# A second modulation mat-vec moved from the Fourier stage into the input projection's tail, and a regrouped Fourier stage

## The reference, cut to what matters

```python
mod_lat = silu(c) @ w_mod + b_mod              # 6*D wide; the first 2*D are needed at once (shift, scale of norm 1)
mod     = silu(c_2) @ w_ada_2 + b_ada_2        # 6*D wide, for the second block

prj = modulate(rmsnorm(x, norm1), sh1, sc1) @ w_in           # z, xbc, dt, f
z, xbc, dt, f = split_proj(prj)
y   = ssd_mixer(z, xbc, dt, ...)                             # conv, silu, scan
fg  = f.reshape(b, l, 4, 128)
spec = fft2(fg, axes=(1, 3), norm='ortho').real              # over 1024 tokens and 128 channels
four = einsum('blgc,gcd->blgd', spec, w_four)
x = x + g1 * (concatenate([y, four]) @ w_out)
```

## Time and profile before

| | before |
|---|---|
| median of 3 runs | 3131.88 us |
| lowest and highest run | 3130.84 and 3138.63 us |
| span of the profiled execution (first to last instruction) | 3136.6 us |
| PE, PEld, DVE, ACT, POOL busy | 90%, 60%, 39%, 20%, 7% |
| mean granted TensorE clock | 0.944 of full speed |

### The profile page before, as it was taken

The page is one execution under the profiler, slowest core; times in us unless marked ns, Lnnn a source line. Parts: engine busy times, 40 slices in busy tenths (PEclk is TensorE's granted clock), DMA queues, the critical chain, the costliest instruction groups (busy, mean ns, idle before and its releaser), DMA issues. The chain is left out here.

```text
span 3136.6 us, 36957 instructions
## 1 busy us (share of the span) xinstructions
PE 2816.6 (90%) x14094; PEld 1878.9 (60%) x14094; DVE 1226.3 (39%) x1848; ACT 639.7 (20%) x1057; POOL 231.0 (7%) x242
## 2 busy tenths in 40 slices
PE   4999996987798899999998599799888899999998
PEld 2888775762576545445544487687666645445444
DVE  3666317885524311111113564673442611111113
ACT  4322323641302000000002422233120200000002
POOL 0000000000000000000002121121000000000002
PEclk6999997998999899999999699899898899999999
DMA  6642226779735799999996413453653699999995
GB/s 246 242 163 71 74 76 198 222 226 422 269 111 204 286 408 410 409 411 406 412 411 227 114 48 108 81 122 111 228 188 130 273 388 412 409 409 406 409 410 215
DMA packets 294747, 812.65 MB, mean 259 GB/s; under 512 B 38364, under 2 KB 160760, under 8 KB 232432
## 3 DMA queue, kind: packets, MB, share of 16 engines
q1 hardware_dynamic: 248864, 702.45, 60.1%
q10 hardware_dynamic: 30640, 62.81, 5.5%
q0 software_dynamic: 15136, 45.91, 4.2%
HBM read 693.18 MB, written 117.91 MB: 259 GB/s over the span
## 5 line engine op out<-in xcount | busy, mean ns | idle before, releaser
L710 PE MATMUL m_ps_y<-m_wa,m_hTa 128*128 128x512 f32 x560 | 255.5, 599 | 0.0
L689 PE MATMUL m_ps_ga<-m_wa,m_xTa 128*128 128x512 f32 x560 | 253.0, 605 | 1.1 <-issue 1.1
L699 PE MATMUL m_ps_b<-m_wb,m_xTb 128*64 128x256 f32 x2240 | 249.5, 381 | 0.0
L689 PE MATMUL m_ps_ua<-m_wa,m_xTa 128*128 128x512 f32 x560 | 246.0, 592 | 0.0
L1145 PE MATMUL xp_acc<-xp_xh,xp_wh 128*128 128x512 f32 (+3 forms) x600 | 223.0, 372 | 6.7 <-DVE xp_xl L1419 6.7
L1146 PE MATMUL xp_acc<-xp_xl,xp_wh 128*128 128x512 f32 (+3 forms) x600 | 221.2, 369 | 0.0
L1147 PE MATMUL xp_acc<-xp_xh,xp_wl 128*128 128x512 f32 (+3 forms) x600 | 221.1, 368 | 0.0
L699 PEld LDWEIGHTS m_ps_b<-m_wb,m_xTb 128*64 128x64 f32 x2240 | 157.8, 137 | 102.3 <-issue 26.5
L812 DVE TENSOR_TENSOR m_hida<-m_ps_ua,m_sila 128x512 f32<-128x512 f32 x35 | 24.2, 691 | 471.1 <-PE m_ps_ua L689 471.1
L780 ACT ACT_TABLE_LOAD x35 | 44.9, 1283 | 756.3 <-PE m_ps_ga L689 675.7
L2379 PE MATMUL xq_acc<-xq_xh,xq_wh 128*128 128x512 f32 x448 | 180.7, 403 | 13.5 <-DVE xq_xl L2801 8.4
(11 more groups left out here) (553 smaller groups left out, 4455.1 us busy)
## 6 DMA issues: line engine op xcount, KB each, us to landing
m_wa<-in_w_dram SPq DMA_DIRECT2D x102, 1024.0 KB, 11.3
m_wb<-in_w_dram SPq DMA_DIRECT2D x102, 1024.0 KB, 12.0
m_wa<-in_w_eg_dram SPq DMA_DIRECT2D x36, 1024.0 KB, 13.1
m_wa<-in_w_eu_dram SPq DMA_DIRECT2D x36, 1024.0 KB, 11.5
m_wb<-in_w_eg_dram SPq DMA_DIRECT2D x36, 1024.0 KB, 11.2
m_wb<-in_w_eu_dram SPq DMA_DIRECT2D x36, 1024.0 KB, 14.6
m_wa<-in_w_ed_dram SPq DMA_DIRECT2D x36, 1024.0 KB
m_wb<-in_w_ed_dram SPq DMA_DIRECT2D x36, 1024.0 KB, 16.1
```

Source lines behind the costliest of these rows:

```text
L689: last = nc.tensor.matmul(out[:, :], xT_a[:, j, :], w[:, k, :], start=(j == 0), stop=(j == J - 1))
L699: last = nc.tensor.matmul(ps_b[c * SB:(c + 1) * SB, p // 2, :], xT_b[:, j, :], w[:, k, c * HF:(c + 1) * HF], start=(j == 0), stop=(j == J ...
L710: last = nc.tensor.matmul(ps_y[:, d * NF:(d + 1) * NF], hT_a[:, k, :], w[:, c, d * NF:(d + 1) * NF], start=(k == 0), stop=(k == JF - 1))
```

## The change

The mat-vec leaves `fourier`, and `mod_tiles` is gone. In `mixer1_in` it is done in ten chunks of 1024 columns (`MC`), eight 128x1024 tiles (512 KB) each, through a ring of four (`MR`). The ring, three accumulators (`macc`) and the result rows (`mrow`) use the SBUF space of the convolution's buffers, which are free after n = 17. For chunk c (M0 = 18):

- SP issues its eight loads in iteration n = 21 + c, after `weights(n)` (`mod_weights`); at n = 21 it also issues eight small bias loads (`mod_biases`); chunks 8 and 9 follow after the loop, then the writes of `a_dram`, then eight stores and the wait for them (`mod_store`). POOL clears `mrow`.
- ACT multiplies the first tile with its silu(c) column (`mod_first`) after the drains of n = 18 + c.
- VectorE adds the other seven, one SCALAR_TENSOR_TENSOR 128x1024 each (`mod_rest`), at the end of iteration n = 18 + c. Each waits for the one before.
- PE sums over the partitions with four matmuls 128x256 against a column of ones (`mod_summed`) after the first group of n = 21 + c, and VectorE adds the bias to the sum (`mod_biased`) in iteration n = 22 + c, before that iteration's `mod_rest`.

The step sizes and decay sums of `mixer1_in` come one iteration earlier (n = 17 and 20 on ACT and VectorE, PE's `sums` at n = 19).

`fourier` loads f by channel group with a semaphore each, loads the twiddle table last and waits for it only ahead of the second matmuls. The first matmuls go group by group in halves of t. The butterflies are done in two halves of 256 columns, each after its own two groups; the copies that turned `t = 6` by -i and the two 128x4096 copies at the end are folded into the operand choice and the sign of `rot`. The second matmuls go by group: 8 x 2 for one group into one of two PSUM slots of 128x1024, then one ACT copy and one VectorE subtraction of 128x1024.

```diff
@@ mixer1_in
+    M0 = Z0 + 1
+        MC, MR, MA = 1024, 4, 3
+        groups = [(k, g) for k, part in enumerate(mod_parts) for g in range(part[1].shape[1] // MC)]
+        NM2 = len(groups)
+        mring, macc, mrow = sb("mring", [P, MR, MC]), sb("macc", [P, MA, MC]), sb("mrow", [P, NM2, MC // NQ4])
...
+        def conv_buffers_free(eng):
+            eng.wait_ge(s_cv, NM)
+            eng.wait_ge(s_xc, NM)
+            eng.wait_ge(s_tq, Q_DT + 1)
+            for r in range(4):
+                eng.wait_ge(s_to[r], 16 * len(range(r, 3 * NT, 4)))
...
+                conv_buffers_free(pool)
+                nc.gpsimd.memset(mrow[:, :, :], 0.0).then_inc(s_mz, 1)
...
+                def mod_weights(c):
+                    k, g = groups[c]
+                    w_m = mod_parts[k][1].rearrange("(p j) n -> p j n", j=J)
+                    if c == 0:
+                        conv_buffers_free(sp)
+                    for j in range(J):
+                        i = J * c + j
+                        if i >= MR:
+                            d, e = divmod(i - MR, J)
+                            if e == 0:
+                                sp.wait_ge(s_m1, d + 1)
+                            else:
+                                sp.wait_ge(s_mf, (J - 1) * d + e)
+                        sp.dma_start(mring[:, i % MR, :], w_m[:, j, g * MC:(g + 1) * MC]).then_inc(s_mw[i % MR], 16)
...
                 for n in range(2, NCH):
                     weights(n)
...
+                    if n >= M0 + 3:
+                        mod_weights(n - M0 - 3)
+                    if n == M0 + 3:
+                        mod_biases()
+                for c in range(NCH - M0 - 3, NM2):
+                    mod_weights(c)
...
                 sp.wait_ge(s_ad, 32)
+                mod_store()
...
+                def mod_summed(c):
+                    pe.wait_ge(s_mf, (J - 1) * (c + 1))
+                    if c < 2:
+                        pe.wait_ge(s_te, Q_SUM + 2 + c)
+                    else:
+                        pe.wait_ge(s_me, c - 1)
+                    n = MC // NQ4
+                    for q in range(NQ4):
+                        last = nc.tensor.matmul(mod_sum(c)[q * CG:q * CG + 1, :], ONE[:, 0:1], macc[:, c % MA, q * n:(q + 1) * n],
+                                                start=True, stop=True)
+                    last.then_inc(s_mr, 1)
...
                 for n in range(2, NCH):
                     for g in range(3 if n <= DT else 2):
                         product(n, g)
+                        if g == 0 and n >= M0 + 3:
+                            mod_summed(n - M0 - 3)
...
-                    if n == DT + 4:
+                    if n == DT + 3:
                         sums()
...
+                def mod_first(c):
+                    i = J * c
+                    if c == 0:
+                        act.wait_ge(s_msg, 1)
+                    act.wait_ge(s_mw[i % MR], 16 * (i // MR + 1))
+                    if c >= MA:
+                        act.wait_ge(s_mr, c - MA + 1)
+                    k = groups[c][0]
+                    nc.scalar.activation(macc[:, c % MA, :], mring[:, i % MR, :], ACT.Copy, scale=msg[:, k, 0:1]).then_inc(s_m1, 1)
...
+                def mod_rest(c):
+                    k = groups[c][0]
+                    v.wait_ge(s_m1, c + 1)
+                    for j in range(1, J):
+                        i = J * c + j
+                        v.wait_ge(s_mw[i % MR], 16 * (i // MR + 1))
+                        nc.vector.scalar_tensor_tensor(out=macc[:, c % MA, :], in0=mring[:, i % MR, :], scalar=msg[:, k, j:j + 1],
+                                                       in1=macc[:, c % MA, :], op0=ALU.mult, op1=ALU.add).then_inc(s_mf, 1)
+                        v.wait_ge(s_mf, (J - 1) * c + j)
...
                     if n + 2 < NCH:
                         low(n + 2)
-                    if n == DT + 2:
+                    if n == DT + 1:
                         step_sizes()
-                    if n == DT + 5:
+                    if n == DT + 4:
                         decay_values()
                     if n == DT + 7:
                         sums_out()
+                    if n >= M0 + 4:
+                        mod_biased(n - M0 - 4)
+                    if n >= M0 and n - M0 < NM2:
+                        mod_rest(n - M0)
+                for c in range(NCH - M0 - 4, NM2):
+                    mod_biased(c)
@@ fourier
-                sp.dma_start(rt[:, :, :, :], rot).then_inc(s_in, 16)
-                sp.dma_start(fT[:, :, :], f_dram).then_inc(s_f, 16)
-                mod_load(sp)
-                mod_store(sp)
+                for g in range(G):
+                    sp.dma_start(fT[:, g, :], f_dram[:, g, :]).then_inc(s_f[g], 16)
+                sp.dma_start(rt[:, :, :, :], rot).then_inc(s_rt, 16)
...
+                for g in range(G):
+                    pe.wait_ge(s_f[g], 16)
+                    for h in range(2):
+                        u = 2 * g + h
+                        if u >= 2:
+                            pe.wait_ge(s_ev, 2 * (u - 1))
+                        for i in range(T // 2):
+                            t = h * (T // 2) + i
+                            last = nc.tensor.matmul(p_u[:, u % 2, i, :, :], fT[:, g, t * P:(t + 1) * P], cw[:, g, :, :],
+                                                    start=True, stop=True)
+                        last.then_inc(s_u, 1)
+                pe.wait_ge(s_rt, 16)
+                for g in range(G):
+                    pe.wait_ge(s_g, g * NB // G + 1)
+                    if g >= 2:
+                        pe.wait_ge(s_ol, g - 1)
+                    for k2 in range(T):
                         for a in range(2):
-                            last = nc.tensor.matmul(p_f[:, k2 % 2, g, :], ab[:, a, k2, g * P:(g + 1) * P], rt[:, a, k2, :],
+                            last = nc.tensor.matmul(p_f[:, g % 2, k2, :], bb[:, a, k2, g * P:(g + 1) * P], rt[:, a, k2, :],
                                                     start=(a == 0), stop=(a == 1))
                     last.then_inc(s_o, 1)
...
+                def butterflies(n):
+                    v.wait_ge(s_ev, 4 * G // NB * (n + 1))
+                    x, y = (z[:, :, :, n * CB:(n + 1) * CB] for z in (ab, bb))
+                    for c in (re, im):
+                        tt(y[:, c, 0:4, :], x[:, c, 0:4, :], x[:, c, 4:8, :], ALU.add)
+                        last = tt(y[:, c, 4:8, :], x[:, c, 0:4, :], x[:, c, 4:8, :], ALU.subtract)
+                    link(last)
...
-                nc.vector.tensor_copy(ab[:, re, :, :], bb[:, re, :, :])
-                nc.vector.tensor_scalar(ab[:, im, :, :], bb[:, im, :, :], -1.0, None, ALU.mult).then_inc(s_g, 1)
...
+                for n in range(NB):
+                    butterflies(n)
+                for g in range(G):
+                    v.wait_ge(s_oe, g + 1)
+                    o = [z[:, g, :].rearrange("p (n k) -> p k n", k=T) for z in (fl, fh)]
+                    nc.vector.tensor_tensor(o[0], p_f[:, g % 2, :, :], o[1].bitcast(F32), ALU.subtract).then_inc(s_ol, 1)
```

More of the change, by code:

```diff
@@ L904, in _ @@
                         nc.vector.tensor_tensor(row[r, g, :], acc[r, g, :], row[r, g, :], ALU.add).then_inc(s_row, 1)
[L907 to L966, removed]
-                last = nc.tensor.matmul(acc[q * CG:q * CG + 1, n % 2, :], sg[:, k, j:j + 1], ring[:, i % R, q, :],
-                                        start=(j == 0), stop=(j == J - 1))
-            last.then_inc(s_mm, 1)
-    def finish(v, n):
-        if n == 0:
-            v.wait_ge(s_b, 16 * NQ4 * len(parts))
-        v.wait_ge(s_mm, J * (n + 1))
-        nc.vector.tensor_tensor(row[:, n, :], acc[:, n % 2, :], row[:, n, :], ALU.add).then_inc(s_row, 1)
-    return clear, load, store, silu, products, finish, len(steps)
@@ L1213, in _ @@
                         sums_turned()
+                for c in range(NCH - M0 - 3, NM2):
+                    mod_summed(c)
             @block.scalar
@@ L1784, in _ @@
                 pe.wait_ge(s_cw, 1)
-                pe.wait_ge(s_f, 16)
-                for t in range(T):
-                    if t >= 2:
-                        pe.wait_ge(s_ev, 2 * (t - 1))
-                    for g in range(G):
-                        last = nc.tensor.matmul(p_u[:, t % 2, g, :, :], fT[:, g, t * P:(t + 1) * P], cw[:, g, :, :],
-                                                start=True, stop=True)
-                    last.then_inc(s_u, 1)
-                    mod_products(pe, t, t + 1)
@@ L1814, in _ @@
-                for k2 in range(T):
-                    act.wait_ge(s_o, k2 + 1)
-                    nc.scalar.activation(fh[:, :, k2::T], p_f[:, k2 % 2, :, :], ACT.Copy).then_inc(s_oe, 1)
+                for u in range(2 * G):
+                    g, t = u // 2, slice(u % 2 * (T // 2), (u % 2 + 1) * (T // 2))
+                    act.wait_ge(s_u, u + 1)
```

(2 more changed lines are left out.)

162 lines of the change are left out of this document (83 added, 79 removed).

## The result

The changed kernel takes 3129.32 us (median of 20 runs, 3126.68 to 3134.37); beside it on the same chips the kernel before took 3134.67 (20 runs, 3130.84 to 3139.26). The ratio is 0.9983, 95% interval 0.9976 to 0.9989: a gain of 5.3 us, where 26 were forecast. It lies above the range and within the 0.3% (9.4 us) that the prediction counted as no change. The two profiled executions stand 7.7 us apart (3136.6 and 3128.9).

A forecast was written before the change was run, and what follows sets the result against it. It took two side-by-side chains, the 40 MB stream and the transform, to hold the Fourier stage. Fourier's -50.7 us and the input stage's +24.7 gave -26.0, from 3131.9 to 3105.9 us; range 3084 to 3127.

The forecast's parts named there:

- the DMA pitch: Input stage: loads plus other traffic set the time per chunk, 13.4 us for chunks 1 to 7.
- the forecast 494.1: Input stage: the scan starts at 494.1 us after sum, bias and stores; the stage grows by 24.7 us.
- The ring rival: Input stage: four slots' round trip adds to other traffic, 15.0 us a chunk; net -12, 3120 us; chance 0.20.
- three in flight cover 3.8 us: Input stage ring: argument against the ring rival, set against 4.4 us to landing.
- The sign to watch: Input stage: DMA share over 0.9 if right; tiles over 1.6 us apart, share well under 0.9 for the ring rival.
- The slower rival: Input stage: landing time grows with load, four slots fail to cover it; 17.8 us a chunk, 3149 us; chance 0.09.
- the hidden rival: Input stage: transfers overlap so well that VectorE's 10.7 us a chunk rules; net -45, 3087 us; chance 0.15.
- Fourier: Fourier stage: earlier start, butterflies in two halves of 34.6 us together, end at 770.9 instead of 821.64; gain 50.7 us.
- VectorE's operation: Input stage: one SCALAR_TENSOR_TENSOR 128x1024 takes 1.27 us, 1.30 with the wait for the one before.

The follow-up runs named there:

- run 2: Changed kernel with VectorE's seven operations a chunk on 64 of 1024 columns, all loads kept, results incomplete: 3087.52 us in all, mat-vec 151.3 us.
- run 5: Changed kernel with a ring of six slots instead of four: 3110.39 us, ratio 0.992 to the kernel before.
- run 1: Changed kernel with a ring of eight slots instead of four: 3105.35 us, ratio 0.99 to the kernel before.
- run 7: Changed kernel with a ring of eight slots, each load bringing two tiles (1 MB): 3105.88 us, ratio 0.9913 to the kernel before.
- run 4: Changed kernel's input stage with the old Fourier transform, no mod products in it: 3151.98 us, ratio 1.0049 to the kernel before.
- run 3: Changed kernel with each mod tile load bringing 64 of 1024 columns, VectorE's work at full width: 3067.09 us in all, mat-vec 129.9 us.
- run 6: Changed kernel, ring of four, bias loads moved to ACT's queue and ACT's first product of chunk 2 ahead of `decay_values`: 3125.53 us, ratio 0.9974.
- run 8: Changed kernel with eight slots, run 6's two moves, and the result's stores split between ACT and SP: 3100.59 us, ratio 0.9893 to the kernel before.

## Why the prediction was wrong

**The step that failed** is the DMA pitch: "DMA. A 512 KB tile is 1.28 us at 410 GB/s" and "I take 13.4 for chunks 1 to 7", with 11.6 for each of the last two. It took the rate that other streams reach and gave it to a ring of four 512 KB slots. Measured: 15.4 and 13.85. The account of the input stage: end of chunk 0 at 366.8 instead of 369.0 (-2.2, of which 1.3 is the earlier start of `low(20)`); chunks 1 to 7 108.0 instead of 93.8 (+14.2); chunks 8 and 9 27.7 instead of 23.2 (+4.5); last bias, stores and stage change 10.0 instead of 8.1 (+1.9). Sum +18.4.

That it is the depth is shown, not only argued: with eight slots chunks 1 to 7 take 12.98 us and the last two 11.4, and the whole 3105.35 us, against the 3105.9 of the prediction. The agreement of the total is luck: there the scan starts 6.4 us before the forecast 494.1 and Fourier is 3.0 shorter than forecast, while that scan is 3.4 longer than before and the rest 1.3; and the profiled span before, 4.7 us above the median of three runs, is only 1.9 above that of twenty. The pitches, 12.98 for 13.4 and 11.4 for 11.6, agree without such help. Five of the kernels with all loads, on one scale. "Under way" is loads of the ring in the stretch x median landing / length, an estimate (for the ring of four: (44 x 5.5 + 22 x 6.0)/122.1 = 3.1 loads); GB/s is of all traffic in the stretch:

| run | slots, load | under way, MB | GB/s | mat-vec, us |
|---|---|---|---|---|
| changed kernel | 4, 512 KB | 1.6 | 346 | 158.5 |
| 2, thin VectorE | 4, 512 KB | 2.0 | 363 | 151.3 |
| 5 | 6, 512 KB | 2.5 | 389 | 141.9 |
| 1 | 8, 512 KB | 3.1 | 399 | 134.6 |
| 7 | 4 x 2, 1 MB | 3.2 | 398 | 137.0 |

What the runs set is the depth of the ring; the bytes under way follow from it and from the landing time, which grows with them. In the changed kernel and in run 7 three loads are under way alike, of 512 KB and of 1 MB, at 346 and 398 GB/s; in runs 1 and 7 as many bytes are, in six loads and in three, at the same rate. So the rate goes with the bytes under way and not with the number of loads. One thing stays open: runs 1 and 7 are both near the 410 GB/s of other slices, where little can differ. Two slots of 1 MB against four of 512 KB, the same 2 MB, were not run. The row that should have warned was there: the old stream reached its 421 GB/s with a ring of five 1 MB slots that took 10.5 us to land, a tile every 2.5 us, that is some 4 MB under way. The change cut the ring from 5 MB to 2 MB. The forecast's pitch left that out; only its rivals weighed it.

**The ring rival** (0.20) named the mechanism: four slots' round trip on top of the other traffic. Its size was near too, +39 in the stage against +43.1. With 4.4 us to landing it had 15.0 and 13.0 a chunk; measured 15.4 and 13.85 with 5.5 to 6.0 us. It was given too small a chance by "three in flight cover 3.8 us", which treats the landing time as fixed. Run 2 shows that it is not.

**The sign to watch was wrong.** The prediction would have taken a DMA share well under 0.9 for the ring's mark, and over 0.9 for a full stream. The share was 0.97 at 346 GB/s and 1.04 at 399. A part of it is that SP's packets took longer: 103 ns each for 2.28 KB in the mean in the changed kernel (16,644 packets, 88.1% of 16 engines over 122.1 us), 99 ns for 2.37 KB with eight slots (15,404, 93.2%, 102.2 us). The other half of its sign held, ring tiles more than 1.6 us apart: 15.4/8 is 1.9.

**The slower rival** did not come in size: it needed 15.9 for each of chunks 1 to 9. The changed kernel has (502.53 - 366.80)/9 = 15.1. But its mechanism, a landing time that grows with the load, is what the runs show (5.5 to 6.0 us for 4.4, where it needed 6.6), and it was near: the move alone, run 4, costs 15 to 17 us.

**The floor of the hidden rival** was too low. It had the scan at 475.0 if transfers hid; with thin loads, run 3, it starts at 483.46, and the 9.0 us of VectorE's waiting for ACT were in no sum.

**Two handoffs**, together 3.9 us by run 6. The eight bias loads were in the sum (3.4 us) but for chunk 0; they hold up chunk 1. ACT's wait for VectorE in `decay_values`, with `mod_first` queued behind it, was missing.

**Fourier** held step by step. First matmul of f 8.0 us after the start (forecast 9.6); butterflies from 16.3 us (18.4), 33.9 long (34.6); the end 66.5 us after the start (70.0), so -54.2 for -50.7. These are the lines of the changed kernel:

```profile
755.35 14.08 PE L1831 MATMUL fo_u<-fo_cw,fo_fT 128*128 128x256 f32 x64 [1.32 <-DVE fo_cw L1860]
...
763.67 4.63 DVE L1865 TENSOR_TENSOR fo_bb<-fo_ab 128x1024 f32<-128x1024 f32 x4 [8.38 <-ACT fo_ab L1851]
...
797.59 3.94 DVE L1903 TENSOR_TENSOR x_fl<-fo_f,x_fh 128x1024 fp32r<-128x1024 f32 x2
799.71 9.82 PE L1841 MATMUL fo_f<-fo_rt,fo_bb 128*128 128x128 f32 x64 [9.81 <-DVE x_fl L1903]
...
811.60 1.99 DVE L1903 TENSOR_TENSOR x_fl<-fo_f,x_fh 128x1024 fp32r<-128x1024 f32 x1 [1.53 <-ACT x_fh L1854]
```

Group 2's matmuls wait for the subtraction after both halves, as foreseen, and 64 of them take 9.82 us, where 5.6 + 4.3 were put down.

**VectorE's** operation was priced right: 1284 ns for 1.27 us. TensorE idled 23 us in the stage (148.5 - 125.2) and did not end last.

**The scan** came out 3.2 us longer. The same instructions took 230.1 to 235.1 us in the eight other profiles (runs 1 to 8: 235.0, 230.1, 234.6, 234.2, 235.1, 232.9, 231.0, 230.5), in no order that follows an edit: thin VectorE 230.1, thin loads 234.6. So 3.2 is not a cost that the runs put on the change. What makes a scan long or short is open.

## What to carry to other kernels

A stream through a ring has to be priced by the bytes that can be under way, so compare slots x size with those of the stream whose rate you borrow, and read GB/s, not the DMA share. Where a stream's consumer waits for tiles while its issuer waits for slots, as here, the ring is too shallow; widen it before touching either side. When small work is woven into a full stage, go through each in-order queue for what stands behind its new waits, the tail's stores included.
